# End of the layers of a transformer encoder with routed experts: adds of stored expert outputs moved, last blocks shared by four engines, a square in halves

## Chip, cores and metric

One core of a Trainium2 chip (trn2) runs the whole program in one launch. The metric is the device time of one execution in microseconds (us). The engines are named as in the profile: PE (TensorE; PEld its weight loads), DVE (VectorE), ACT (ScalarE), POOL (GpSimd) and SP (SyncE, which only issues transfers here). Everything is float32.

## What is computed

Two layers over 512 tokens of width 1024, then a final RMSNorm. What matters here is how a layer ends:

```python
for l in range(DEPTH):
    ...
    x = x + g1 * hybrid_mixer(h, ...)
    h = rms_norm(x, norm2[l]) * (1.0 + sc2) + sh2
    x = x + g2 * grouped_moe(h.reshape(B * S, D), w_router, router_bias,
                             w1[l], w3[l], w2[l]).reshape(B, S, D)
return rms_norm(x, norm_f)
```

`grouped_moe` sends each token to two of 16 experts and adds their two outputs with weights `gw`. The next layer begins with `rms_norm(x, norm1)`.

## The kernel before

The tokens are four blocks `t` of 128 rows; `x[:, t, :]` is 128 x 1024. The routed part of a layer runs in eleven passes (`PASSES`) of 128 token places each. In a pass PE multiplies gathered tokens with w1 and w3 of the pass's experts (`up_tiles`, L2130), ACT and DVE form the hidden values, PE transposes them (`hidden_transposes`, L2116) and multiplies by w2 (`down_tiles`, L2141) in two halves of 512 columns, into banks 6 and 7. DVE scales each half by `g2` into `ysb` (`put_out`, L1637) and counts it on `y_e`. For passes 0 to 9 POOL scatters `ysb` to the array `ys_d` in HBM, two rows for each token. When the scatters have landed, SP loads `ys_d` back, 1 MB for each block, into `cy[t]` (`load_outputs`, L773): blocks 0 and 1 into `reg_a`, 2 and 3 into `reg_b`. DVE adds them to `x` with the weights (`add_output`, L1185: one scalar_tensor_tensor of 128 x 1024 for each of the two outputs; `add_outputs` is both).

The last pass isn't stored. PE adds it straight from `ysb` by a product with a matrix `last_t` that holds places and weights (`last_pass`, L1757), into the banks that `last_bank` names.

- After layer 0, DVE adds these banks to `x` (`add_last_pass`, L1199) and ACT squares block after block for the norm of layer 1 (`square`, L934; `root`, L938). DVE makes mean squares (`mean_square`, L1173), reciprocals (L1178) and the scaled rows `xn` (L1180), which PE transposes (L1775).
- After layer 1, PE also adds `x` itself by a product with the identity (L1756), so the final `x` of a block lies in two banks. ACT squares each half there (L1151), DVE works out the mean square (L1704, L1707), ACT the root (L938), DVE the reciprocal (L1709) and the two scaled halves (L1713), and SP stores the block (L802). `fx_s` tells PE that a block of `x` is ready.

All orders are written out by hand: each engine has one program, in which it waits on counting semaphores. The order of DVE at the end of a layer is that of its last step (`e == PASSES`): the stored outputs of block 0, the two halves of the last down product, then (layer 0 only) one stored output of block 1. A conditional piece (`extra_blocks`) for routings that overflow the passes stands between the passes and the last adds on every engine; with these inputs none of its instructions runs, only the branch. PE waits for both halves of `y_e` ahead of that branch.

## Time and profile before

| | |
|---|---|
| median of 3 runs | 1547.74 us (1547.10 to 1547.87) |
| the profiled execution's own time | 1547.94 us |
| its span, first to last instruction | 1546.0 us |
| mean granted TensorE clock | 0.982 |
| PE busy | 1461.4 us, 95% of the span |
| DVE, ACT, POOL busy | 615.0, 427.2 and 87.1 us (40%, 28%, 6%) |
| chain of waits that ended last | PE 87%, DMA 6%, DVE 3%, ACT 2%, issue 1% |
| moved by the transfer engines | 346.8 MB, mean 224 GB/s |

The profile is of one execution. The chain of waits follows the last instruction back to whatever released it, so its shares say on what the end hung. All times in the rows are from the start of the span. Layer 0 ends around 770 to 782 us, layer 1 at 1518 to 1546 us.

### The profile page before, as it was taken

Reading aid. Unit: us, or ns where it says so; the run is one execution under the profiler, and the core shown is the slowest. Engines: PE = TensorE matmul, PEld = TensorE weight load, DVE = VectorE, ACT = ScalarE, POOL = GpSimd, SP = SyncE. Lnnn points to the kernel's source line nnn. Section 1 sums busy time; section 2 is a strip of 40 time slices with the busy share of each in tenths; the row PEclk is TensorE's granted clock in tenths of the full one; section 3 lists DMA queues with packets and bytes.
Section 4 is the critical chain, followed back from the end, with each engine's and each line's share of the span. In section 5 each row is a group of like instructions: output and inputs, shape, how many; then the busy total and the mean of one; then the engine's idle time right before and its main releaser. Section 6 shows DMA issues by size and latency. Waiting matters only on the chain.

```text
span 1546.0 us, 19921 instructions
## 1 busy us (share of the span) xinstructions
PE 1461.4 (95%) x7688; PEld 797.8 (52%) x7689; DVE 615.0 (40%) x1395; ACT 427.2 (28%) x988; POOL 87.1 (6%) x96
## 2 busy tenths in 40 slices
PE   4998999999999799999899899999999969999997
PEld 1565555677754443343346555666776433333333
DVE  0377554565742511111165774464333251111115
ACT  1427565300011211111141565541000122111112
POOL 0000002000000101100000000110000010111000
PEclk8999999999999799999999999999999979999999
DMA  9626073225282799999972703401303368999994
GB/s 361 243 84 247 2 247 107 83 67 151 65 316 97 287 372 392 421 419 422 375 272 109 243 35 122 151 1 41 109 1 152 148 231 340 407 408 420 424 413 188
DMA packets 94874, 346.80 MB, mean 224 GB/s; under 512 B 13738, under 2 KB 37898, under 8 KB 80376
## 3 DMA queue, kind: packets, MB, share of 16 engines
q1 hardware_dynamic: 69152, 305.68, 50.8%
q0 software_dynamic: 8976, 31.40, 5.5%
q10 hardware_dynamic: 16648, 8.40, 1.9%
q8 instruction: 63, 1.03, 0.3%
q14 instruction: 35, 0.29, 0.1%
HBM read 331.55 MB, written 21.00 MB: 228 GB/s over the span
## 4 chain that ended last, share of the span: by engine, by line
PE 87%; DMA 6%; DVE 3%; ACT 2%; issue 1%; DVEq 0%; SPq 0%; POOLq 0%; ACTq 0%
PE bank L2130 18%; PE bank L1868 13%; PE bank L1811 10%; PE bank L2141 9%; PE bank L2036 7%; PE bank L1910 7%; PE bank L1925 5%; PE bank L1935 4%; PE bank L1945 4%; DMA ring<-in_w 3%; PE bank L1851 2%; PE bank L1775 2%; DMA ring<-in_w_ada 1%; PE bank L1740 1%; PE bank L2096 1%
## 5 line engine op out<-in xcount | busy, mean ns | idle before, releaser
L2130 PE MATMUL bank<-ring,reg_b 128*32 128x512 f32 (+2 forms) x1312 | 269.0, 602 | 2.1 <-ACT reg_b L1113 2.1
L1811 PE MATMUL bank<-ring,hT 128*128 128x512 f32 (+3 forms) x512 | 158.9, 471 | 2.4 <-ACT hT L946 2.4
L2130 PEld LDWEIGHTS bank<-ring,reg_b 128*32 128x32 f32 (+2 forms) x1312 | 86.4, 125 | 139.7 <-issue 136.9
L2141 PE MATMUL bank<-ring,reg_b 128*32 128x512 f32 (+2 forms) x768 | 141.5, 594 | 6.8 <-DMA ring<-in_w 5.4
L1811 PEld LDWEIGHTS bank<-ring,hT 128*128 128x128 f32 x512 | 97.7, 192 | 59.0 <-issue 32.2
L1910 PE MATMUL bank<-reg_a,ring 128*128 128x512 f32 x256 | 112.6, 593 | 0.9 <-issue 0.9
L2036 PE MATMUL bank<-ring,reg_b 128*128 128x512 f32 x256 | 113.0, 596 | 0.0
L1113 ACT ACTIVATE reg_b<-bank,cur 128x128 f32<-128x128 f32 x176 | 64.0, 470 | 164.9 <-PE bank L2096 164.9
L1025 ACT ACTIVATE reg_f<-bank,nmax 128x512 f32<-128x512 f32 x128 | 87.2, 684 | 57.2 <-DVE nmax L1337 56.1
L1337 DVE TENSOR_REDUCE nmax<-bank 128x1 f32<-128x512 f32 x128 | 83.7, 685 | 47.9 <-PE bank L1925 47.7
L2141 PEld LDWEIGHTS bank<-ring,reg_b 128*32 128x32 f32 (+2 forms) x768 | 47.6, 123 | 78.7 <-issue 76.1
L1868 PE MATMUL bank<-hT,ring 128*128 128x256 f32 x384 | 88.1, 379 | 0.0
L1637 DVE TENSOR_TENSOR reg_d<-bank,reg_c 128x512 f32<-128x512 f32 x44 | 30.3, 691 | 138.5 <-PE bank L2141 138.5
L2130 PE MATMUL bank<-hT,reg_b 128*32 128x512 f32 (+2 forms) x288 | 84.6, 593 | 0.0
L1868 PEld LDWEIGHTS bank<-hT,ring 128*128 128x128 f32 x384 | 72.8, 190 | 15.8 <-issue 6.7
L1945 PE MATMUL bank<-cst,reg_f 128*128 128x128 f32 x512 | 71.8, 282 | 7.9 <-DVE reg_f L1331 5.1
L1625 DVE TENSOR_TENSOR reg_b<-bank,reg_b 128x512 f32<-128x512 f32 x22 | 15.2, 692 | 159.0 <-ACT reg_b L1120 159.0
L1910 PEld LDWEIGHTS bank<-reg_a,ring 128*128 128x128 f32 x256 | 48.5, 190 | 55.6 <-issue 54.9
L2036 PEld LDWEIGHTS bank<-ring,reg_b 128*128 128x128 f32 x256 | 47.7, 190 | 56.3 <-issue 56.3
L1331 DVE TENSOR_SCALAR reg_f<-reg_f,linv 128x512 f32<-128x512 f32 x128 | 66.2, 517 | 10.3 <-issue 0.4
L1945 PEld LDWEIGHTS bank<-cst,reg_f 128*128 128x128 f32 x512 | 55.4, 142 | 28.1 <-DVE reg_f L1331 18.8
L1630 DVE TENSOR_TENSOR reg_b<-bank,reg_b 128x512 f32<-128x512 f32 x22 | 15.2, 692 | 123.6 <-PE bank L2130 123.6
(305 smaller groups left out, 1832.8 us busy)
## 6 DMA issues: line engine op xcount, KB each, us to landing
ring<-in_w SPq DMA_DIRECT2D x72, 2048.0 KB, 15.4
ring<-in_w_ada SPq DMA_DIRECT2D x19, 2048.0 KB, 11.8
reg_a<-in_w SPq DMA_DIRECT2D x12, 2048.0 KB, 12.7
hT<-in_w SPq DMA_DIRECT2D x12, 2048.0 KB, 15.6
ring<-in_w_in SPq DMA_DIRECT2D x10, 2048.0 KB, 19.3
vb<-in_w_ada ACTq DMA_DIRECT2D x16, 512.0 KB, 3.9
ring<-in_w_o SPq DMA_DIRECT2D x4, 2048.0 KB, 8.1
ring<-in_w_proj_a SPq DMA_DIRECT2D x8, 512.0 KB, 10.7
```

What stands on the lines that cost most here:

```text
L1025: A(prob[:, u % 2, h, :], bank[4 + at][:, :], ACT.Exp, bias=nmax[:, at:at + 1], accum_out=lsum[:, at:at + 1]).then_inc(ex_s, 1)
L1113: ins = A(xsT[:, b, cc, :], bank[(p0 + k) % 2][:, c * P:(c + 1) * P], ACT.Identity, scale=scale2(cc), bias=shift2(cc))
L1331: TS(prob[:, u % 2, h, :], prob[:, u % 2, h, :], linv[:, at:at + 1], None, ALU.mult).then_inc(pn_s, 1)
L1337: v.tensor_reduce(nmax[:, at:at + 1], bank[4 + at][:, :], X, ALU.max, negate=True).then_inc(mx_s, 1)
L1811: ins = pe.matmul(bank[z_bank(k)][:, 0:n], hT[:, c, t * P:(t + 1) * P], w[:, c, :], start=c == 0, stop=c == NC - 1)
L1868: ins = pe.matmul(bank[bk][:, half * 256:(half + 1) * 256], w[:, c, :], tokens[:, c, :], start=c == 0, stop=c == 3)
L1910: ins = pe.matmul(branch_bank(j, q)[:, :], w[:, c, (j % 4) * P:(j % 4 + 1) * P], oT[:, c + 4 * q, :], start=c == 0, stop=c == 3)
L1925: pe.matmul(bank[4 + 2 * (u % 2) + h][:, :], q_of(k, h), k_of(k, h), start=True, stop=True).then_inc(s_r, 1)
L1945: ins = pe.transpose(bank[2 + h][:, kc * P:(kc + 1) * P], prob[:, u % 2, h, kc * P:(kc + 1) * P], ident)
L2036: ins = pe.matmul(wo_bank(k)[:, :], mT[:, c, t * P:(t + 1) * P], w[:, c, :], start=c == 0, stop=c == NC - 1)
L2130: ins = pe.matmul(bank[bk][at:at + n, :], xsT[:, p % 2, c, at:at + n], slot(MOE_SLOT[j, m], NC, F)[:, c, :], start=c == 0, stop=c == NC - 1)
L2141: ins = pe.matmul(bank[6 + h][at:at + n, :], uT[:, c, at:at + n], slot(MOE_SLOT[j, 2], 4, D)[:, c, h * 512:(h + 1) * 512], start=c == 0, s ...
```

## The change

1. The stored outputs of block 0 are added between the two halves of the last down product (in the last layer those of block 1 too, after them), where they stood ahead of both halves.
2. PE's wait for `ysb` is taken per half, inside `last_pass`, and stands behind the branch.
3. In the last layer only blocks 0 and 2 get `x` through the identity product; for both halves this stands ahead of the two `last_t` products. In blocks 1 and 3 DVE adds the banks to `x` (`final_add`). Block 3's stored outputs are weighted by ACT (in place), summed and added to `x` by POOL. Block 3 is loaded ahead of block 2.
4. Of the final scaling ACT does three halves (block 0, and half 0 of block 2), whose gain POOL multiplies in; DVE does the other five. The last block is stored in two halves.
5. In the norm at the start of layer 1, block 0 is squared in two halves, the first as soon as its half of `x` is there.

```diff
 def last_bank(layer, t):
-    return ((6, 2, 6, 6) if layer < DEPTH - 1 else (6, 2, 4, 0))[t]
+    return ((6, 2, 6, 6) if layer < DEPTH - 1 else (2, 4, 0, 6))[t]
 ...
 # SP
-                for t in range(2, NT):
+                for t in (2, 3) if l < DEPTH - 1 else (3, 2):
                     load_outputs(t, cg_s[t])
 ...
+            t = NT - 1
+            for h in range(2):
+                cols = slice(h * 512, (h + 1) * 512)
+                wait(sp, out_s[t], h + 1)
+                sp.dma_start(out[0, t * P:(t + 1) * P, cols], xn[:, t, cols]).then_inc(out_st, 16)
 ...
 # POOL
+                if l == DEPTH - 1:
+                    both = cy[NT - 1]
+                    wait(pool, fw_s, 2)
+                    pool.tensor_tensor(both[:, 0, :], both[:, 0, :], both[:, 1, :], ALU.add).then_inc(fp_s, 1)
+                    wait(pool, fp_s, 1)
+                    pool.tensor_tensor(x[:, NT - 1, :], x[:, NT - 1, :], both[:, 0, :], ALU.add).then_inc(fp_s, 1)
+                    wait(pool, fp_s, 2)
                 extra_blocks(pool, rows_beyond(pool, l), n_ov, n_tab, body, new_table)
                 pool.sem_inc(ov_all, 1)
+            for n, (t, h) in enumerate(((0, 0), (0, 1), (2, 0))):
+                cols = slice(h * 512, (h + 1) * 512)
+                wait(pool, fy_s, n + 1)
+                pool.tensor_tensor(xn[:, t, cols], xn[:, t, cols], nf_row[:, cols], ALU.mult).then_inc(out_s[t], 1)
 ...
 # ACT
+                    if l > 0 and t == 0:
+                        act.wait_ge(xh_s, l)
+                        A(sq_j[:, 0:512], x[:, t, 0:512], ACT.Square, accum_out=ssq_h[:, 0:1]).then_inc(sqz_s, 1)
+                        act.wait_ge(x2, l * NT + 1)
+                        A(sq_j[:, 512:D], x[:, t, 512:D], ACT.Square, accum_out=ssq[:, t:t + 1]).then_inc(sq_s, 1)
 ...
+                if l == DEPTH - 1:
+                    act.wait_ge(cg_s[NT - 1], l * 16 + 16)
+                    for k in range(2):
+                        A(cy[NT - 1][:, k, :], cy[NT - 1][:, k, :], ACT.Identity, scale=gw[:, k, NT - 1:NT]).then_inc(fw_s, 1)
                 extra_blocks(act, most, n_ov, n_tab, body)
             warm_root(DEPTH + 1)
 ...
             for t in range(NT):
-                for h, (total, done) in enumerate(((lsum, sqh_s), (ssq, sq_s))):
-                    act.wait_ge(lp_r, ((DEPTH - 1) * NT + t) * 2 + h + 1)
-                    A(sq_j[:, h * 512:(h + 1) * 512], bank[last_bank(DEPTH - 1, t) + h][:, :], ACT.Square,
-                      accum_out=total[:, t:t + 1]).then_inc(done, 1)
+                for h in range(2):
+                    final_square(t, h)
+                    if t == 3 and h == 0:
+                        final_scale(2, 0)
                 root(2 * DEPTH, t)
+                if t == 0:
+                    for h in range(2):
+                        final_scale(0, h)
 ...
 # DVE
-                    else:
-                        add_outputs(l, 0)
-                        out_before()
-                        if l < DEPTH - 1:
-                            add_output(l, 1, 0)
+                    elif l < DEPTH - 1:
+                        out_before((0,))
+                        add_outputs(l, 0)
+                        out_before((1,))
+                        add_output(l, 1, 0)
+                    else:
+                        add_outputs(l, 0).then_inc(fx_s, 1)
+                        out_before((0,))
+                        add_outputs(l, 1)
+                        out_before((1,))
 ...
+            add_outputs(DEPTH - 1, 2).then_inc(fx_s, 1)
+            final_add(1, 0)
+            final_root(0)
+            final_add(1, 1)
+            final_root(1)
+            v.drain()
+            for h in range(2):
+                final_out(1, h)
+            v.wait_ge(fp_s, 2)
+            final_add(3, 0)
+            final_root(2)
+            final_add(3, 1)
+            v.drain()
+            final_out(2, 1)
+            final_root(3)
+            v.drain()
+            for h in range(2):
+                final_out(3, h)
 ...
 # PE, last_pass
-                for h in range(2):
-                    cols = slice(h * 512, (h + 1) * 512)
-                    own = layer == DEPTH - 1
-                    dst = bank[last_bank(layer, t) + h][:, :]
-                    if own:
-                        pe.matmul(dst, ident, x[:, t, cols], start=True, stop=False)
-                    pe.matmul(dst, last_t[:, t, :], ysb[:, 0, cols], start=not own, stop=True).then_inc(lp_r, 1)
+                if own:
+                    for h in range(2):
+                        pe.matmul(dst[h], ident, x[:, t, cols[h]], start=True, stop=False)
+                for h in range(2):
+                    if t == 0:
+                        pe.wait_ge(y_e, (layer * PASSES + PASSES) * 2 - 1 + h)
+                    pe.matmul(dst[h], last_t[:, t, :], ysb[:, 0, cols[h]], start=not own, stop=True).then_inc(lp_r, 1)
```

`own` is true for blocks 0 and 2 of the last layer. `final_square(t, h)` squares a half from its bank (even `t`) or from `x` (odd `t`); `final_root(t)` is the mean square, the wait for ACT's root and the reciprocal as before; `final_out(t, h)` is the scaling by reciprocal and gain, from `x` for odd `t` and from the bank for even `t`; `final_scale(t, h)` is ACT's scaling by the reciprocal alone.

DVE at the very end of the last layer, before (L1185 stored outputs, L1637 halves of the last down product, L1704 to L1713 the norm of block 0):

```order
L1185 SCALAR_TENSOR_TENSOR x<-reg_a,gw,x 128x1024 [waits token_outputs_loaded0] x2
L1637 TENSOR_TENSOR reg_d<-bank,reg_c 128x512 [waits expert_out_ready,expert_out_stored0]
L1637 TENSOR_TENSOR reg_d<-bank,reg_c 128x512 [waits expert_out_ready]
...
L1185 SCALAR_TENSOR_TENSOR x<-reg_a,gw,x 128x1024 [waits token_outputs_loaded1] x2
L1185 SCALAR_TENSOR_TENSOR x<-reg_b,gw,x 128x1024 [waits token_outputs_loaded2] x2
L1704 TENSOR_SCALAR lsum<-lsum 128x1 [waits square_sum_of_first_half]
L1707 TENSOR_SCALAR ssq<-ssq,lsum 128x1 [waits square_sums]
L1709 RECIPROCAL rstd<-ssq 128x1 [waits roots]
L1713 SCALAR_TENSOR_TENSOR reg_a<-bank,rstd,reg_c 128x512 x2
L1185 SCALAR_TENSOR_TENSOR x<-reg_b,gw,x 128x1024 [waits token_outputs_loaded3] x2
```

And now (L1249 stored outputs, L1703 halves, L1772 `final_add`, L1777 to L1782 `final_root`, L1788 `final_out`):

```order
L1249 SCALAR_TENSOR_TENSOR x<-reg_a,gw,x 128x1024 [waits token_outputs_loaded0] x2
L1703 TENSOR_TENSOR reg_d<-bank,reg_c 128x512 [waits expert_out_ready,expert_out_stored0]
L1249 SCALAR_TENSOR_TENSOR x<-reg_a,gw,x 128x1024 [waits token_outputs_loaded1] x2
L1703 TENSOR_TENSOR reg_d<-bank,reg_c 128x512 [waits expert_out_ready]
...
L1249 SCALAR_TENSOR_TENSOR x<-reg_b,gw,x 128x1024 [waits token_outputs_loaded2] x2
L1772 TENSOR_TENSOR x<-bank4,x 128x512 [waits last_pass_added_up]
L1777 TENSOR_SCALAR lsum<-lsum 128x1 [waits square_sum_of_first_half]
L1780 TENSOR_SCALAR ssq<-ssq,lsum 128x1 [waits square_sums]
L1782 RECIPROCAL rstd<-ssq 128x1 [waits roots]
L1772 TENSOR_TENSOR x<-bank5,x 128x512 [waits last_pass_added_up]
```

The pair for block 1 went between the halves, the pair for block 3 left DVE, and two adds from banks came in.

PE at the same place, before (L1756 identity, L1757 last pass; each row is one half of a block, block 0 and the start of block 1 shown; the branch waits for `expert_out_read`, which is `y_e`):

```order
L533 COMPARE_AND_BRANCH [waits expert_out_read]
...
L1756 MATMUL bank6<-x,cst 128x512 [waits final_x_in_sbuf,last_pass_weights_copied]
L1757 MATMUL bank6<-reg_d 128x512
L1756 MATMUL bank7<-x,cst 128x512
L1757 MATMUL bank7<-reg_d 128x512
L1756 MATMUL bank2<-x,cst 128x512 [waits final_x_in_sbuf]
```

And now (L1849 identity, L1853 last pass; block 0 in banks 2 and 3, block 1 in 4 and 5, block 2 in 0 and 1; block 3 follows):

```order
L541 COMPARE_AND_BRANCH
...
L1849 MATMUL bank2<-x,cst 128x512 [waits final_x_in_sbuf,last_pass_weights_copied]
L1849 MATMUL bank3<-x,cst 128x512
L1853 MATMUL bank2<-reg_d 128x512 [waits expert_out_read]
L1853 MATMUL bank3<-reg_d 128x512 [waits expert_out_read]
L1853 MATMUL bank4<-reg_d 128x512
L1853 MATMUL bank5<-reg_d 128x512
L1849 MATMUL bank0<-x,cst 128x512 [waits final_x_in_sbuf]
L1849 MATMUL bank1<-x,cst 128x512
L1853 MATMUL bank0<-reg_d 128x512
...
```

The sixteen half-block products became twelve, and the wait for `ysb` moved from the branch to the products that read it.

DVE between the layers, now (L1263 the last pass's halves into `x`, L1231 and L1234 the mean square of block 0 in two steps; before it was one step, L1173, and nothing stood between the two halves of L1637):

```order
L1703 TENSOR_TENSOR reg_d<-bank,reg_c 128x512 [waits expert_out_ready,expert_out_stored0]
L1249 SCALAR_TENSOR_TENSOR x<-reg_a,gw,x 128x1024 [waits token_outputs_loaded0] x2
L1703 TENSOR_TENSOR reg_d<-bank,reg_c 128x512 [waits expert_out_ready]
L1249 SCALAR_TENSOR_TENSOR x<-reg_a,gw,x 128x1024 [waits token_outputs_loaded1]
...
L1263 TENSOR_TENSOR x<-bank,x 128x512 [waits last_pass_added_up] x2
L1249 SCALAR_TENSOR_TENSOR x<-reg_a,gw,x 128x1024 [waits token_outputs_loaded1]
L1231 TENSOR_SCALAR ssq_h<-ssq_h 128x1 [waits square_sum_of_first_half_after_moe]
L1234 TENSOR_SCALAR ssq<-ssq,ssq_h 128x1 [waits square_sums]
```

The stored outputs of block 0 now follow the first half; the rest keeps its place.

## Rows read from the trace of the kernel before

**Rows 1.** Chain of waits, last 30 us (start us, us, what).

```profile
1517.88 7.15 PE bank L2141 x16
...
1525.06 0.08 DVE reg_d L1637
...
1525.28 0.52 DVEq L1697
...
1526.17 1.10 PE bank L1756 x2
...
1539.28 0.87 PE bank L1757 x2
...
1540.18 0.70 ACT reg_f L1151 x2
```

**Rows 2.** Timeline, end of layer 1 (start us, us, engine, line, out<-in, count).

```profile
1517.85 1.28 ACT L961 ACT_TABLE_LOAD   x1
...
1521.69 0.69 DVE L1637 TENSOR_TENSOR reg_d<-bank,reg_c 128x512 f32<-128x512 f32 x1 [0.48 <-PE bank L2141]
...
1525.88 2.64 DVE L1185 SCALAR_TENSOR_TENSOR x<-reg_a,gw,x 128x1024 f32<-128x1024 f32 x2
...
1533.27 2.63 DVE L1185 SCALAR_TENSOR_TENSOR x<-reg_b,gw,x 128x1024 f32<-128x1024 f32 x2
...
1541.62 1.41 DVE L1713 SCALAR_TENSOR_TENSOR reg_a<-bank,rstd,reg_c 128x512 f32<-128x512 f32 x2
```

**Rows 3.** Chain of waits between the layers and in layer 1.

```profile
807.00 43.25 PE bank L1811 x148
...
1469.53 7.05 PE bank L2130 x64
...
1477.89 23.60 DMA ring<-in_w
```

**Rows 4.** Timeline between the layers.

```profile
767.88 2.41 PE L2141 MATMUL bank<-ring,reg_b 128*128 128x512 f32 x5 [0.69 <-ACT reg_b L1125]
...
771.99 2.65 DVE L1185 SCALAR_TENSOR_TENSOR x<-reg_a,gw,x 128x1024 f32<-128x1024 f32 x2 [5.51 <-DMA reg_a<-ys_d]
...
774.56 1.28 DVE L1637 TENSOR_TENSOR reg_d<-bank,reg_c 128x512 f32<-128x512 f32 x2
...
776.32 3.70 PE L1757 MATMUL bank<-reg_d 128*128 128x512 f32 x8 [1.30 <-DVE reg_d L1637]
...
777.03 0.16 DVE L1216 COPY gain<-gain_n 128x8 f32<-128x8 f32 x1
...
778.34 0.69 DVE L1199 TENSOR_TENSOR x<-bank,x 128x512 f32<-128x512 f32 x1 [0.17 <-PE bank L1757]
...
778.95 1.28 DVE L1185 SCALAR_TENSOR_TENSOR x<-reg_a,gw,x 128x1024 f32<-128x1024 f32 x1
...
780.25 0.15 DVE L1173 TENSOR_SCALAR ssq<-ssq 128x1 f32<-128x1 f32 x1
```

**Rows 5.** Transfers: issue of the loads of blocks 2 and 3, and us to landing of both.

```profile
1515.86 0.80 SPq L773 DMA_DIRECT2D reg_b<-ys_d  x2
...
DMA to landing us min/median/max: 8.2/9.3/10.3
```

**Rows 6.** Timeline, POOL and DVE in layer 1's attention.

```profile
1004.73 0.49 DVE L1331 TENSOR_SCALAR reg_f<-reg_f,linv 128x512 f32<-128x512 f32 x1
...
1004.79 2.63 POOL L849 TENSOR_TENSOR ring<-hT,ring 128x1024 f32<-128x1024 f32 x1 [0.18 <-POOL hT L847]
...
1005.59 2.12 DVE L1331 TENSOR_SCALAR reg_f<-reg_f,linv 128x512 f32<-128x512 f32 x1
...
1007.60 2.34 POOL L851 TENSOR_TENSOR ring<-hT,ring 128x1024 f32<-128x1024 f32 x1 [0.18 <-POOL ring L849]
```

**Rows 7.** Line L1104 on ACT: durations in ns min/median/max, first and last start.

```profile
L1104 ACT ACTIVATE reg_a<-x,rstd x2: 1132/1132/1132, 504.4 to 1253.7; 128x1024 f32<-128x1024 f32 x2
```

**Rows 8.** Transfers, final stores: KB each, median us to landing.

```profile
out<-reg_a SPq DMA_DIRECT2D x4, 512.0 KB, 2.6
```

More of the change, by code:

```diff
@@ L513, in trunk @@
         ov_all = sem("extra_pass_done")
-        out_s = sem("out_ready")
+        out_s = [sem(f"out_block_{t}_ready") for t in range(NT)]
         out_st = sem("out_stored")
@@ L799, in _ @@
                 wait(sp, y_r, (l * PASSES + PASSES) * 2)
-            for t in range(NT):
-                wait(sp, out_s, t + 1)
+            for t in range(NT - 1):
+                wait(sp, out_s[t], 2)
                 sp.dma_start(out[0, t * P:(t + 1) * P, :], xn[:, t, :]).then_inc(out_st, 16)
-            wait(sp, out_st, 16 * NT)
+            t = NT - 1
[3 more added lines that the diff above has]
+                sp.dma_start(out[0, t * P:(t + 1) * P, cols], xn[:, t, cols]).then_inc(out_st, 16)
+            wait(sp, out_st, 16 * (NT + 1))
         @block.gpsimd
@@ L1171, in mean_square @@
             def mean_square(base, t):
+                if base in range(2, 2 * DEPTH, 2) and t == 0:
+                    v.wait_ge(sqz_s, base // 2)
+                    TS(ssq_h[:, 0:1], ssq_h[:, 0:1], 1.0 / D, EPS, ALU.mult, ALU.add)
+                    v.drain()
+                    v.wait_ge(sq_s, base * NT + (t + 1))
+                    TS(ssq[:, t:t + 1], ssq[:, t:t + 1], 1.0 / D, ssq_h[:, 0:1], ALU.mult, ALU.add).then_inc(ms_s, 1)
+                    return
                 v.wait_ge(sq_s, base * NT + (t + 1))
@@ L1630, in hidden, with put_out @@
                     TT(u_s, bank[5][:, :], u_s, ALU.mult).then_inc(u_s_s, 1)
-                def put_out(f, p):
-                    for n in range(2):
+                def put_out(f, p, halves=(0, 1)):
+                    for n in halves:
                         v.wait_ge(y_r, (l * PASSES + f) * 2 + (n + 1))
@@ L1694, in _ @@
                 extra_blocks(v, most, n_ov, n_tab, body, new_table, finish=add_extra)
[L1697 to L1714 removed]
+                v.drain().then_inc(xe_s, 1)
@@ new lines, in final_add, with final_root @@
+            def final_add(t, h):
+                v.wait_ge(lp_r, ((DEPTH - 1) * NT + t) * 2 + h + 1)
+                cols = slice(h * 512, (h + 1) * 512)
+                TT(x[:, t, cols], bank[last_bank(DEPTH - 1, t) + h][:, :], x[:, t, cols], ALU.add).then_inc(fa_s, 1)
+            def final_root(t):
+                v.wait_ge(sqh_s, DEPTH + t + 1)
+                TS(lsum[:, t:t + 1], lsum[:, t:t + 1], 1.0 / D, EPS, ALU.mult, ALU.add)
+                v.drain()
+                v.wait_ge(sq_s, 2 * DEPTH * NT + t + 1)
+                TS(ssq[:, t:t + 1], ssq[:, t:t + 1], 1.0 / D, lsum[:, t:t + 1], ALU.mult, ALU.add).then_inc(ms_s, 1)
+                v.wait_ge(rt_s, 2 * DEPTH * NT + (t + 1))
+                v.reciprocal(rstd[:, t:t + 1], ssq[:, t:t + 1]).then_inc(fr_s, 1)
@@ L1746, in last_pass @@
                     pe.wait_ge(wt_s, layer + 1)
[L1747 to L1749 removed]
+                own = layer == DEPTH - 1 and t % 2 == 0
+                if own:
+                    pe.wait_ge(fx_s, t // 2 + 1)
+                elif layer < DEPTH - 1 and t >= 2:
                     pe.wait_ge(x2, (layer + 1) * NT + (1 if t == 2 else 3))
[L1751 to L1757 removed]
+                dst = [bank[last_bank(layer, t) + h][:, :] for h in range(2)]
+                cols = [slice(h * 512, (h + 1) * 512) for h in range(2)]
+                if own:
+                    for h in range(2):
+                        pe.matmul(dst[h], ident, x[:, t, cols[h]], start=True, stop=False)
+                for h in range(2):
+                    if t == 0:
+                        pe.wait_ge(y_e, (layer * PASSES + PASSES) * 2 - 1 + h)
+                    pe.matmul(dst[h], last_t[:, t, :], ysb[:, 0, cols[h]], start=not own, stop=True).then_inc(lp_r, 1)
             pe.wait_ge(clr_s, 1)
```

66 lines of the change are left out of this document (39 added, 27 removed).

## The prediction

> **What bounds the kernel now.** I read the page's totals, then the chain of waits, then the timelines of the two places that the change touches, last the transfers and POOL. PE is busy for 95% of the span and carries 87% of the chain, so only what takes work or a wait off PE's path, or shortens the tail behind PE, can count. At the end of layer 1 [rows 1] the reader is to see four things. The last down product takes 7.15 us from 1517.88. PE then does nothing until 1526.17: DVE still reads the second half (to 1525.75), and PE's branch stands behind the wait for it. Sixteen half-block products of 0.86 us follow without a gap, to 1540.15. A tail of ACT and DVE for the last block ends it at 1543.03 [rows 1, 2]; one store of 512 KB, 2.6 us to landing [rows 8], and the close of the program reach 1546.0. Between the layers [rows 4] PE ends its last-pass products at 780.02 and then waits for DVE and ACT, which go through two adds from the banks, a square, mean, root and scaling; the mean square ends at 780.40. From 807 on PE is the chain [rows 3], and of the late loads the longest, 23.60 us from 1477.89, is issued when PE's product at 1469.53 has ended. So an earlier start of layer 1 moves the loads with it, and I carry a gain there in full to the end.
>
> **Between the layers.** DVE's first half of the down product is ready at about 771.7 (767.88 and the 3.81 us that layer 1 has from the product's start to DVE's read, 1517.88 to 1521.69 [rows 1, 2]), so it goes ahead of the stored outputs at no cost but 0.3 us on a pair that has slack until 775.0. The second half then starts at 775.06 and ends at 775.75, against the pair's end at 775.84 [rows 4]. PE has its branch behind it and the first half's `ysb`, so its products start at 775.0 to 775.4, not at 776.32, and both halves are done when DVE has copied its gains (777.19, less 0.1). DVE's two adds, the second of which waited for PE until 778.34, run back to back from 777.15 to 778.46; before they ended at 779.03: 0.57 us. The split square ends some 0.8 us after the adds, about 779.3, where the whole one ended just ahead of DVE's step at 780.25; but DVE still has the stored output of block 1 in front of the mean square (1.28 us from 778.95, now from 778.38 to 779.66), then two small steps of 0.15 and 0.22 in place of one. The mean square is there at 780.02, not 780.40. Everything behind waits for it: **0.38 us gained**. Bounds: 0.1 (PE's products come late after all) and 0.6 (the adds' gain in full).
>
> **The last layer, with no engine disturbing another.** The second down half isn't delayed: block 0's pair ends at 1521.2, the first half takes 1521.69 to 1522.38 [rows 2], block 1's pair 2.64 us, to 1525.0, and the second half is ready at 1525.03. PE needs only `x` of block 0 for its identity products, so they start when the down product has been issued. I take 1525.0; the branch, 0.42 us from 1525.75 to 1526.17 in rows 1, could push it to 1525.4. Twelve products of 0.86 end at 1535.5, against 1540.15. But the loads set a second date: block 3's outputs land 8.2 us after 1515.86, at 1524.06, block 2's at 1516.24 + 10.3 = 1526.54 [rows 5]. DVE's pair for block 2 then runs to 1529.2; PE wants it at 1530.2. Then DVE and ACT are the path. Block 1's first half is added by 1530.3, block 0's root and reciprocal end at 1531.1, ACT scales block 0 to 1532.4 (two of about 0.65) and squares block 1 to 1533.7; root and reciprocal to 1534.3, DVE's two halves of block 1 to 1535.7 (0.67 each from SBUF), the add of block 3's first half to 1536.35, block 2's mean, root and reciprocal to 1537.2, the second add to 1537.8, DVE's half of block 2 to 1538.65. ACT meanwhile squares and scales to 1538.95, and mean, root, reciprocal and two halves end at **1541.0**. That is 2.0 us before 1543.03. The gain on PE (4.6 us) is not on the path by then: DVE is late next. It gives up one pair (2.6 us) and three scalings (0.7 each), but takes four adds from banks (0.7 each), and it still waits for ACT's root four times.
>
> **The last store.** Its second half is 256 KB. A load of 1 MB behind another took 2.1 us longer [rows 5] (10.3 - 8.2, issued 0.4 apart, so 2.5 for 1 MB), so 256 KB less are worth about 0.6 us; I take **0.45**, with bounds of 0 and 0.7.
>
> **What POOL takes back.** ACT weights block 3's outputs in two steps of 1.13 us [rows 7] from 1524.06, done at about 1526.25; POOL then runs two adds of 128 x 1024, 2.34 us each [rows 6]. Rows 6 show what that does to DVE: a tensor_scalar on SBUF takes 0.49 us, but the one that starts at 1005.59 under POOL's add takes 2.12 and ends 0.3 us after the add; POOL's own add, begun under a DVE instruction, takes 2.63 in place of 2.34. One holds the other off for a whole instruction. No row shows the form at stake here, a scalar_tensor_tensor that reads two tensors in SBUF (DVE's pair for block 2), so its hold lies between 0 and all of POOL's time; I take it as held, since the nearest row is. The Trainium skill (SBUF — State Buffer, Who interferes with whom) says that a DVE instruction with two SBUF inputs contends with a GpSimd instruction that reads SBUF, as an exclusive lock; by it the hold is certain (the rows don't show this form), and the adds from a bank, with one SBUF input, go free. If the two alternate once, the pair for block 2 ends at 1531.2 instead of 1529.2, and what hung at 1529.6 moves by 1.6 us. POOL's gain products (about 1.2 us each, half of 2.34) then touch DVE's scaling of block 1, 0.3 more. **1.9 us lost**, DVE ends at 1542.9.
>
> **Sum.** -0.38 - 2.0 - 0.45 + 1.9 = -0.9 us, against the profiled execution's 1547.94: 1547.0. The median of the runs is 0.2 below that execution, so the forecast is 1546.8.
>
> **Rivals.**
> - *No hold.* POOL and DVE don't meet: 1547.74 - 2.85 = 1544.9. For it: rows 6 show only a single-tensor instruction held. Against: they show no SBUF-reading DVE instruction that ran through a POOL add. A further 0.3 from PE's early start, a full 0.7 at the store or 0.6 between the layers takes it past 0.2%.
> - *Held twice, slower than before.* POOL's first add starts at about 1526.4, 0.15 us before block 2 has landed. It decides here: if POOL is first, DVE's first step of the pair waits until 1528.7 and ends at 1529.8; POOL's second add, waiting since 1528.9, slips in before the second step, which ends at 1533.2. PE's products for block 2 start 3 us late, DVE's chain 3.6 us; POOL is out of the way afterwards. End of DVE 1544.45: 1547.74 + 1.4 - 0.45 - 0.38 = 1548.3. For it: the dates above. Against: 0.15 us is within what landings move, and the gap between the pair's two steps is under 0.1 us. Past 0.2% it would take another 2.5 us, as by small DVE steps held too (1.6 us each time).
> - *The early start doesn't come about.* PE's branch and waits hold its products until after 1526. Then the end loses up to 1 us only where nothing is held: 1545.9.
>
> **How the numbers follow.** About 0.2% (3.1 us) is what a measurement of this kernel can tell from no change. Forecast 0.45, no hold 0.27, held twice 0.18, late start 0.06, the rest for mishaps of either sign. The range reaches from the no-hold case with its bounds, 1544.3, to held twice with the late bounds, 1549.0. Faster by over 0.2% is half of the no-hold case: 0.14. Slower by over 0.2%: 0.04. Within: 0.82.
>
> **What would show it.** Between the layers: DVE's two adds back to back, and the mean square about 0.4 us sooner after the down product's start. At the end: identity products at 1525 on the old clock; POOL's first add beside DVE's pair for block 2, one step of which takes over 2 us; DVE's last scaling 25.0 us after the down product's start (25.15 before), 23.1 with no hold, 26.6 if held twice. It would be wrong if DVE's pair takes 2.6 us under POOL's add, if the last store gains nothing, or if PE's stretch in layer 1 changes length.

## The result, and the profile after

| | before | after |
|---|---|---|
| median of the runs | 1547.74 us | 1552.71 us |
| lowest to highest, 7 runs each | 1547.10 to 1550.81 | 1551.12 to 1557.37 |
| ratio after / before | | 1.0031, 95% interval 1.0019 to 1.0043 |
| profiled execution, its span | 1547.94 / 1546.0 us | 1557.37 / 1555.6 us |

The change makes the kernel slower by 5.0 us, 0.31%. The forecast was 1546.8 with a range up to 1549.0, and it gave 0.04 to slower by over 0.2%: it was wrong in sign, and the time lies outside its range. In the comparisons below three executions that took 1691 to 4807 us (two of e2, one of e10b) are left out.

The profiled execution of after is the slowest of its seven, so it has to be read by pieces. All times below are counted from the start of a layer's **last down product** (before 767.88 and 1517.88, after 772.56 and 1523.52). Ahead of the first of these after is 4.7 us late, in stages that the diff leaves as they were: PE waited 3.30 us for a weight load there (1.79 in before's trace) and ran slowly for some microseconds. The medians are 5.0 apart, not 9.4, and e3 below, which has the same code there, waited 1.78 us; so I count that piece as one of this execution, not of the change.

Timeline of after, PE, the wait ahead of the change:

```profile
754.60 0.62 PE L2237 MATMUL bank<-ring,reg_b 128*32 128x512 f32 x2 [3.30 <-DMA ring<-in_w]
```

**Between the layers.** Timeline of after (columns as in [rows 4]):

```profile
772.56 7.13 PE L2237 MATMUL bank<-ring,reg_b 128*128 128x512 f32 x16 [0.69 <-ACT reg_b L1156]
779.53 3.79 PE L1853 MATMUL bank<-reg_d 128*128 128x512 f32 x8
...
782.06 1.29 DVE L1263 TENSOR_TENSOR x<-bank,x 128x512 f32<-128x512 f32 x2
...
784.68 0.21 DVE L1234 TENSOR_SCALAR ssq<-ssq,ssq_h 128x1 f32<-128x1 f32 x1
...
786.21 1.97 PE L1871 MATMUL bank<-cst,reg_a 128*128 128x128 f32 x8 [2.89 <-DVE reg_a L1244]
...
787.98 2.53 PE L1853 MATMUL bank<-reg_d 128*128 128x512 f32 x4
```

and the same place in before:

```profile
781.72 1.16 PE L1775 MATMUL bank<-cst,reg_a 128*128 128x128 f32 x8 [1.70 <-DVE reg_a L1180]
782.72 1.88 PE L1757 MATMUL bank<-reg_d 128*128 128x512 f32 x4
```

PE's first last-pass products come 6.97 us after the down product's start (8.44 before, [rows 4]), DVE's two adds run back to back (1.29 us), the mean square is there at 784.90, 12.34 us after the start, against 12.52. That is what was forecast (0.38 us), if smaller: 0.18 us. But PE has the same work done earlier and waits for DVE for 2.89 us, where it waited 1.70, and its next eight transposes take 1.97 us, not 1.16, and the four products 2.53, not 1.88. Windows of after (us, busy times of the engines with counts, granted clock of PE, DMA):

```profile
784.56:786.06 1.50, 0.00 (x0) 0.00 (x0) 1.07 (x4) 0.20 (x1) 0.00 (x0) 0.93 1.08 363
786.06:787.56 1.50, 1.35 (x7) 1.35 (x8) 1.24 (x5) 0.13 (x1) 0.00 (x0) 0.50 1.06 373
787.56:789.06 1.50, 1.50 (x5) 0.98 (x5) 1.50 (x2) 1.50 (x5) 0.00 (x0) 0.50 1.06 371
789.06:790.56 1.50, 1.50 (x4) 0.68 (x4) 1.43 (x2) 1.50 (x5) 0.00 (x0) 0.93 1.08 381
```

The granted clock is 0.50 behind the gap (the 1.2 GHz level; 2.4 GHz is 1.00), where in before the eight transposes and four products ran in the times of a clock of 1.00. Layer 1's first product with weights is at 790.51 in the chain of waits, 17.95 us after the down product's start; in before it was at 784.60, 16.72. So this place **loses 1.23 us** in this execution.

**The last layer.** Timeline of after; SPq rows are DMA issues:

```profile
1529.38 2.19 ACT L1179 ACTIVATE reg_b<-reg_b,gw 128x1024 f32<-128x1024 f32 x2 [5.92 <-DMA reg_b<-ys_d]
1530.49 1.88 PE L1849 MATMUL bank<-x,cst 128*128 128x512 f32 x4
...
1531.76 2.34 POOL L931 TENSOR_TENSOR reg_b<-reg_b 128x1024 f32<-128x1024 f32 x1 [14.85 <-ACT reg_b L1179]
...
1532.77 5.69 DVE L1249 SCALAR_TENSOR_TENSOR x<-reg_b,gw,x 128x1024 f32<-128x1024 f32 x2 [1.39 <-DMA reg_b<-ys_d]
...
1534.27 3.10 POOL L933 TENSOR_TENSOR x<-x,reg_b 128x1024 f32<-128x1024 f32 x1 [0.18 <-POOL reg_b L931]
...
1538.51 1.98 PE L1849 MATMUL bank<-x,cst 128*128 128x512 f32 x4 [2.71 <-DVE x L1249]
...
1543.65 5.35 SPq L810 DMA_DIRECT2D out<-reg_a  x3
...
1547.32 1.26 POOL L941 TENSOR_TENSOR reg_a<-reg_a,reg_c 128x512 f32<-128x512 f32 x1 [3.76 <-ACT reg_a L1200]
...
1548.52 1.41 DVE L1788 SCALAR_TENSOR_TENSOR reg_a<-x,rstd,reg_c 128x512 f32<-128x512 f32 x2
1549.37 0.99 SPq L815 DMA_DIRECT2D out<-reg_a  x2
```

PE starts block 0 at 6.97 us after the down product's start (8.29 before, [rows 1]): the early start came. DVE's pair for block 2, 2.64 us where nothing disturbs it, takes 5.69. The chain of waits shows how (start us, us, what):

```profile
1521.87 10.88 DMA reg_b<-ys_d
1532.75 0.03 issue
1532.77 2.41 DVE x L1249
...
1535.25 3.21 DVE x L1249
```

POOL's first add had begun at 1531.76, 1 us before block 2 landed; DVE's first step waits it out and ends at 1535.18, POOL's second add slips in, and DVE's second step ends at 1538.46. DVE's last scaling ends at 1549.93, 26.41 us after the down product's start, against 25.15: **1.26 us lost**. (The trace shows that DVE's steps end behind POOL's adds; that POOL holds DVE is read from the lengths here and tested in e4.)

**The close.** What each engine's end-of-program drain shows in after (durations in ns min/median/max, first and last start in us):

```profile
L208 POOLq DRAIN  x1: 8084/8084/8084, 1547.3 to 1547.3; - x1
...
L208 SPq DRAIN  x1: 13/13/13, 1552.7 to 1552.7; - x1
```

and in before:

```profile
L208 POOLq DRAIN  x1: 7027/7027/7027, 1511.0 to 1511.0; - x1
...
L208 SPq DRAIN  x1: 13/13/13, 1545.8 to 1545.8; - x1
```

SP's drain marks the last store's landing. In before the program ends 0.2 us later. In after POOL is not done then: its drain starts when its last product is issued (1547.3), includes that product (1.26 us) and goes on 6.8 us more, to 1555.4, and the program waits. From DVE's last scaling to the end of the span it is 5.67 us, 2.97 in before: **2.70 us lost**. Nor do the halves of the last store gain anything here: 2.8 us from DVE's end to SP's drain, as before.

The sum is 1.23 + 1.26 + 2.70 = 5.2 us, less 0.27 in layer 1's stretch (from the first product, 790.51, to the last down product 733.01 us, 733.28 before), against the 5.0 us between the medians. Each of these pieces is read from one execution of each kernel; the first of them does not come in every execution, as e3 shows below, so that the sum meets the medians this closely is in part luck.

### The profile page after: what moved, and what is told of

Its sections match the earlier page's. It is cut to its first block, busy times and chain, and to the rows that moved or that the text cites. A ratio compares the mean times of both kernels' runs of the same rounds, so it can differ in the third digit from the quotient of the medians.

```text
span 1555.6 us, 19927 instructions
## 1 busy us (share of the span) xinstructions
PE 1461.6 (94%) x7680; PEld 798.0 (51%) x7681; DVE 616.9 (40%) x1395; ACT 431.7 (28%) x995; POOL 96.3 (6%) x101
## 4 chain that ended last, share of the span: by engine, by line
PE 86%; DMA 6%; DVE 3%; ACT 2%; issue 1%; DVEq 0%; SPq 0%; POOLq 0%; ACTq 0%
PE bank L2226 18%; PE bank L1964 12%; PE bank L1907 10%; PE bank L2237 9%; PE bank L2132 7%; PE bank L2006 7%; PE bank L2021 5%; PE bank L2031 4%; PE bank L2041 4%; DMA ring<-in_w 3%; PE bank L1947 2%; PE bank L1871 2%; DMA ring<-in_w_ada 1%; PE bank L1833 1%; PE bank L2192 1%
## 5 line engine op out<-in xcount | busy, mean ns | idle before, releaser
L1703 DVE TENSOR_TENSOR reg_d<-bank,reg_c 128x512 f32<-128x512 f32 x44 | 30.4, 692 | 145.0 <-PE bank L2237 144.8
```

## Experiments

Every run below was timed beside the kernel before. Ratios are to before. "Filler" is two products on PE that nobody needs, shown under e13.

| run | what it is | ratio, 95% interval |
|---|---|---|
| after | | 1.0031, 1.0019 to 1.0043 |
| e1, e14 | before + the part between the layers | 1.0008, 0.9997 to 1.0019; 1.0015, 1.0004 to 1.0025 |
| e13 | e1 + filler on PE | 1.0002, 0.9993 to 1.0012 |
| e2 | after, the part between the layers undone | 1.0022, 1.0013 to 1.0031 |
| e3 | after, no late product on POOL | 1.0016, 1.0007 to 1.0024 |
| e4 | after, POOL waits for DVE's pair | 1.0014, 1.0005 to 1.0023 |
| e5 | before + one tiny late product on POOL | 1.0029, 1.0018 to 1.0040 |
| e6 | before + one late wait on POOL | 1.0023, 1.0014 to 1.0033 |
| e7 | e3 and e4 together | 1.0000, 0.9990 to 1.0009 |
| e8 | e7 + filler | 0.9990, 0.9981 to 0.9999 |
| e9b | e8, POOL does its two adds alone | 0.9983, 0.9974 to 0.9991 |
| e10b | e9b without the filler | 0.9999, 0.9989 to 1.0008 |
| e11b | after + filler | 1.0032, 1.0020 to 1.0044 |
| e12b | before + last store in halves | 0.9999, 0.9990 to 1.0007 |

### The close of the program: e3, e5, e6

Theory: POOL needs 6.8 to 7 us to close behind whatever it did last. Rival: the stores at the end, 1 MB in a row on the queue. e3 takes the product for block 2, POOL's last, off POOL:

```diff
-            for n, (t, h) in enumerate(((0, 0), (0, 1), (2, 0))):
+            for n, (t, h) in enumerate(((0, 0), (0, 1))):
...
-                    if t == 3 and h == 0:
-                        final_scale(2, 0)
...
+            final_out(2, 0)
             final_out(2, 1)
```

> The changed kernel, but DVE scales half 0 of block 2, so that POOL's last instruction is the gain product of block 0's second half. Theory (the program ends with POOL's drain, 6.8 us after POOL's last arithmetic): POOL's drain ends before the last store has landed, the span ends 0.3 us after that landing (3 us after it in the changed kernel), DVE ends 0.5 us later; in all 2.1 us below the changed kernel, 2.9 above the kernel before. Rival (the end of the program is late for another reason, such as the two half stores): the 3 us stay and the time is 5 us above.

Drains of e3:

```profile
L208 POOLq DRAIN  x1: 9062/9062/9062, 1534.2 to 1534.2; - x1
...
L208 SPq DRAIN  x1: 13/13/13, 1545.6 to 1545.6; - x1
```

POOL is closed at 1543.3 and the span ends at 1545.9, 0.3 us after the landing. DVE has one step more and the hold is still there (pair 5.71 us), so DVE ends 27.3 us after the down product's start, 0.9 us later than in after where 0.5 was expected; the time falls from 1.0031 to 1.0016, 2.3 us. e5 and e6 put the cost alone on the kernel before, whose stores they leave as they are:

```diff
                 pool.sem_inc(ov_all, 1)
 
+            wait(pool, out_s, 4)
+            pool.tensor_tensor(kr[:, 0, 0:8], kr[:, 0, 0:8], kr[:, 0, 8:16], ALU.mult)
```

(e6 has the wait alone.)

> The kernel before, with one thing more: at its end POOL waits until all four blocks are scaled and then does one product of 128 x 8 elements, which nobody needs. Theory (POOL closes only some 6.8 us after its last instruction; the profile of after has a drain of 8.08 us from 1547.3, 1.26 us of it the product): POOL's drain ends at about 1543.1 + 0.1 + 6.8 to 7 = 1550.0, the program ends there, 4 us later than before (ratio about 1.0026). Rival (what after loses at its end comes from the 1 MB of stores that stand in a row on the queue): the time stays at that of before, 1.000, since the stores are not touched and the small product is done long before the last store has landed.

> As e5, but POOL only waits, and does no product. If it is the arithmetic that the drain waits out, POOL's drain is short or starts 7 us before the end unseen, and the time is that of before (1.000); if the drain of POOL takes 7 us whatever it did last, the end comes at 1543.1 + 7.0 = 1550.1, 4 us later (1.0026). I give the second 0.6, since before drains for 7.03 us after an instruction that also moved nothing large.

POOL's product and drain in e5:

```profile
1545.00 0.20 POOL L919 TENSOR_TENSOR kr<-kr 128x8 f32<-128x8 f32 x1 [31.94 <-DVE reg_a L1716]
```

```profile
L208 POOLq DRAIN  x1: 7009/7009/7009, 1545.0 to 1545.0; - x1
L208 SPq DRAIN  x1: 13/13/13, 1547.6 to 1547.6; - x1
```

and POOL's drain in e6:

```profile
L208 POOLq DRAIN  x1: 6769/6769/6769, 1540.7 to 1540.7; - x1
```

A product of 0.2 us that nobody needs costs 4.5 us (0.29%), and a bare wait costs nearly as much (0.23%), with stores untouched: the rival falls. From DVE's last scaling to the end of the span the profiles have 7.4 us in e5 and 7.1 in e6, 2.97 in before. The 6.8 to 7.0 us lie behind POOL's last instruction, of either kind; what POOL does in them stays open. In the kernel before, POOL's drain of 7.03 us begins at 1511.0 and is over by 1518, unseen.

### POOL and DVE: e4

```diff
                     wait(pool, fw_s, 2)
+                    wait(pool, fx_s, 2)
                     pool.tensor_tensor(both[:, 0, :], both[:, 0, :], both[:, 1, :], ALU.add).then_inc(fp_s, 1)
```

> The changed kernel, but POOL begins its two adds only when DVE's pair of block 2 is done. Theory (DVE's pair is held off by POOL's adds): the pair takes 2.6 us instead of 5.7, PE starts block 2's products at once, and DVE's last scaling ends 24 to 25 us after the start of the last down product (26.4 in the changed kernel), since POOL's gain products now meet DVE's scaling of block 1. POOL's drain still ends the program: 1.5 to 2.5 us below the changed kernel, 2.5 to 3.5 above the kernel before. Rival (the pair is slow by itself, beside the loads): it stays at 5.7 us.

Timeline of e4:

```profile
1530.77 2.64 DVE L1250 SCALAR_TENSOR_TENSOR x<-reg_b,gw,x 128x1024 f32<-128x1024 f32 x2 [1.78 <-DMA reg_b<-ys_d]
...
1533.60 2.35 POOL L932 TENSOR_TENSOR reg_b<-reg_b 128x1024 f32<-128x1024 f32 x1 [19.08 <-DVE x L1250]
...
1536.13 2.35 POOL L934 TENSOR_TENSOR x<-x,reg_b 128x1024 f32<-128x1024 f32 x1 [0.18 <-POOL reg_b L932]
```

With nothing else changed the pair is back at 2.64 us and both adds at 2.35. DVE ends at 1544.93, 23.80 us after its down product's start of 1521.13 (26.41 in after, 24 to 25 expected). POOL is now later, its three products end at 1543.72, and its drain still ends the program. The ratio of 1.0014 says 2.6 us gained, as 26.41 - 23.80 does. The Trainium skill (SBUF — State Buffer, Who interferes with whom) calls the pair of ports that DVE and GpSimd share "an exclusive lock" and names a DVE instruction with two SBUF inputs among those that contend. It adds that "issue order, not op shape, decides who blocks". The traces agree with the lock: 5.69 us under POOL's adds (5.71 in e3, 5.82 in e2, 6.62 in e11b), 2.64 without (e4, e7, e8, e9b). On the order they show one side only: POOL's first add began ahead of DVE's pair in all four, by 1.01 us in after and by 0.08 in e11b, and DVE waited each time; no run has DVE's pair begin first under POOL's adds.

### The clock between the layers: e1, e2, e13, e14

e1 and e14 are one kernel, before with this part of the change alone; e2 is after without it:

```diff
-                        out_before((0,))
-                        add_outputs(l, 0)
-                        out_before((1,))
+                        add_outputs(l, 0)
+                        out_before()
                         add_output(l, 1, 0)
...
-                    if l > 0 and t == 0:
+                    if False:
...
-                if base in range(2, 2 * DEPTH, 2) and t == 0:
+                if False:
...
+                if l < DEPTH - 1:
+                    pe.wait_ge(y_e, (l * PASSES + PASSES) * 2)
+
                 def extra_added():
```

> The kernel before with the change's part between the layers alone. Theory (the longer idle of PE lets its clock fall): PE's first transposes of layer 1 run at the granted clock 0.5, as in the changed kernel (eight in 1.97 us, not 1.16), the first product of layer 1 starts 17.9 us after the start of the last down product of layer 0 (16.7 before), and the time is 0.8 to 1.2 us above the kernel before. Rival (the prediction's step): 16.3 us, and 0.4 us below.

> The changed kernel with the order, the waits and the whole square of before between the layers. Theory: 16.7 us from the last down product of layer 0 to layer 1's first product, clock 1.0 there, about 1.2 us below the changed kernel, so 3.8 us above the kernel before. Rival (the loss lies in the unchanged stages, whose loads came later in the changed kernel's profile): still 5 us above.

In e1's profile the theory failed at first. PE waited 2.76 us and no clock fell (the eight transposes took 1.16 us, layer 1's first product stood 16.39 us after the down product, 0.33 under before):

```profile
781.60 1.16 PE L1797 MATMUL bank<-cst,reg_a 128*128 128x128 f32 x8 [2.76 <-DVE reg_a L1195]
```

After and e4 (gaps of 2.89 and 2.9 us) did show the fall, and both had also run at half clock some 25 us before, so I thought the two falls linked. e13 is e1 with the filler; it puts two products behind the first two blocks' last ones, into a bank that nobody reads:

```diff
                     last_pass(l - 1, 1)
+                    for _ in range(2):
+                        pe.matmul(bank[5][:, :], ident, ysb[:, 0, 0:512], start=True, stop=True)
                 norm_transposes(TR_N1, 0, 0)
```

> Before with the part between the layers and the two filler products alone. Theory (of six profiled executions with a gap of 2.8 to 3.1 us between the layers, the three that had run at half clock some 25 us earlier, behind a wait for a load at 752 to 755, ran at half clock behind the gap too, and the other three did not; with the filler none of three did): the first product of layer 1 starts 16.3 to 16.4 us after the last down product (16.72 before, 17.9 with the fall) whatever the load did, and the ratio is 0.9997. Rival (the filler does nothing for the median): the same ratio as e14.

> The kernel of e1 a second time, beside e13 on the same chip. Theory: in a share of its executions the clock falls behind the gap, 1.5 us each time, so it lies 0.3 to 1.5 us above e13 and at 1.0000 to 1.0008 of before. In the profile: if PE waited over 2.3 us for the load at about 752, a granted clock of 0.5 behind the gap and 17.8 to 17.9 us to the first product; if under 2.0 us, a clock of 1.00 and 16.3 to 16.4 us. Rival: no difference from e13, or a fall without the early one.

Timeline of PE in e14, the same kernel as e1:

```profile
751.37 0.62 PE L2163 MATMUL bank<-ring,reg_b 128*32 128x512 f32 x2 [2.79 <-DMA ring<-in_w]
```

```profile
781.10 1.97 PE L1797 MATMUL bank<-cst,reg_a 128*128 128x128 f32 x8 [2.70 <-DVE reg_a L1195]
782.86 2.77 PE L1779 MATMUL bank<-reg_d 128*128 128x512 f32 x4
```

and its windows:

```profile
752.00:754.00 2.00, 2.00 (x25) 0.69 (x20) 0.00 (x0) 0.00 (x0) 0.00 (x0) 1.00 0.99 414
...
782.00:784.00 2.00, 2.00 (x7) 1.48 (x7) 2.00 (x3) 1.69 (x5) 0.00 (x0) 0.50 1.06 373
```

Timeline of PE in e13:

```profile
779.10 1.88 PE L1812 MATMUL bank<-reg_d,cst 128*128 128x512 f32 x4
781.95 1.16 PE L1797 MATMUL bank<-cst,reg_a 128*128 128x128 f32 x8 [0.97 <-DVE reg_a L1195]
782.94 1.88 PE L1779 MATMUL bank<-reg_d 128*128 128x512 f32 x4
```

In e14 the clock is 1.00 at 752 and 0.50 behind a gap of 2.70 us: the fall does not need an earlier one, and by the chain layer 1's first product is at 785.63, 18.00 us after the down product's start (767.63). In e13 it is at 784.83, 16.32 us after 768.51. The means of the 12 times of e14 and of e13 differ by 1.8 us (0.6 to 3.1 by resampling them); e10b against e9b, the same edit elsewhere, gives 2.4 (1.0 to 3.7), e7 against e8 1.0 (-0.1 to 2.1), and after against e11b, below, nothing (1.0031 and 1.0032). So the filler gains clearly in two of the four pairs. That it does so by the clock is shown in the profiles, one of each kernel, and argued for the medians.

Over all profiles: of the seven executions with a gap of 2.70 to 3.07 us (after, e1, e3, e4, e7, e10b, e14) four ran at 0.50 behind it (after, e4, e10b, e14); of the nine whose gap is before's 1.70 or is filled (0.97 to 1.78 left) (before, e2, e5, e6, e8, e9b, e11b, e12b, e13) none did. What decides among the seven stays open: e1 and e14 are one kernel with gaps of 2.76 and 2.70, and e3 and after have 2.89 both.

e2's profile has 16.70 us from the down product's start to the first product (before 16.72), as expected, and its time is 1.4 us below after's by the ratios (1.0022) where 1.2 was expected; the two intervals overlap, so the times alone don't show it.

### After with the filler alone: e11b

> After with nothing but the filler. Theory: the stretch between the layers is 0.2 to 0.3 us shorter than before's in every execution, with a clock of 1.00; the last layer (pair of 5.7 us, DVE's end 26.4 us after the down product's start) and POOL's drain are as in after; 3.5 to 4.2 us above before, ratio 1.0023 to 1.0027. Rival (the fall of the clock has nothing to do with that gap): as after, 1.0031, or a clock of 0.5 there in the profile.

The part between the layers is as expected (16.53 us, clock 1.00), and still the ratio is that of after (1.0032 where 1.0023 to 1.0027 was expected; the interval reaches down to 1.0020). The profile says where it went, in this execution: DVE's pair is held for 6.62 us, DVE ends 27.5 us after the down product's start, and PE's next gap has the fall of the clock instead.

```profile
1527.74 6.62 DVE L1249 SCALAR_TENSOR_TENSOR x<-reg_b,gw,x 128x1024 f32<-128x1024 f32 x2 [1.51 <-DMA reg_b<-ys_d]
...
1534.42 3.47 PE L1849 MATMUL bank<-x,cst 128*128 128x512 f32 x4 [3.76 <-DVE x L1249]
```

Four identity products take 3.47 us, not 1.88, at a granted clock of 0.50. e2 shows the same there (3.48 us behind 3.09 us of gap); after and e3, with gaps of 2.71 and 2.99 us at this place, kept 1.00. Whether that holds for the medians, one profile can't say.

### Both mendings, and a kernel that beats both: e7, e8, e9b, e10b, e12b

> After, with both mendings of the last layer: POOL's adds wait until DVE's pair for block 2 has ended, and DVE, not ACT and POOL, scales the first half of block 2; the part between the layers is after's. Theory: pair for block 2 takes 2.64 us, POOL's last arithmetic ends 8 us or more before the program's end, so its drain is hidden and the program ends 0.3 us after the last store's landing; DVE's last scaling ends 24.0 to 24.8 us after the last down product's start (before 25.15, after 26.41). Sum against before: between layers -0.3 (clock stays) or +1.2 (clock falls), end -0.4 to -1.1: ratio 0.999 to 1.000; clearly under after. Rival (the end holds something else, as the queue of stores): still 2 us or more above before.

> As e7, and PE does two products of 128 x 512 into a free bank, which nobody reads, behind the first two blocks' last products in the gap between layers (2.9 us long there, 1.7 in before). Theory (the clock falls when that gap is long, in some executions): the gap is 1.7 us again, PE's transposes start as in e7 and the clock is 1.00 in every execution there; the median is below e7's by 0 to 1.5 us, by the share of executions in which the clock fell. Rival (the fall comes from something that happens before, as the wait for a DMA at 754): no difference, or +0.1.

e7 (the diffs of e3 and e4) is level with before, e8 with the filler 0.10% under it. DVE ends 23.40 and 24.00 us after the down product's start, where 24.0 to 24.8 was expected. POOL's last product in e7 ends 7.0 us before the program does, not 8 or more, so its drain is only just hidden (to 1544.0, as the last landing). Between the layers e8 shows 1.00 but gains nothing (17.13 us to the first product): DVE waited 0.52 us for block 1's first stored output to land there, a second way in which that part depends on a load. And the stores now pile up, in e7 and in e8. Timeline of e8, SP's queue:

```profile
1538.25 1.65 SPq L810 DMA_DIRECT2D out<-reg_a  x3
1540.54 1.83 SPq L815 DMA_DIRECT2D out<-reg_a  x2
```

Block 0 waits for POOL's product (behind its adds), and blocks 1 and 2 stand behind block 0's store on SP's queue: 2 MB issued between 1538.25 and 1541.2, and the last landing is 3.8 us after DVE's end (1541.11 to 1544.9). POOL's drain ends at 1545.0 too. So e9b takes block 0 back from ACT and POOL and puts it where DVE waited 1.35 us for ACT's squares:

```diff
-            for n, (t, h) in enumerate(((0, 0), (0, 1))):
-                cols = slice(h * 512, (h + 1) * 512)
-                wait(pool, fy_s, n + 1)
-                pool.tensor_tensor(xn[:, t, cols], xn[:, t, cols], nf_row[:, cols], ALU.mult).then_inc(out_s[t], 1)
...
-                if t == 0:
-                    for h in range(2):
-                        final_scale(0, h)
...
             final_add(1, 1)
+            v.drain()
+            for h in range(2):
+                final_out(0, h)
             final_root(1)
```

> As e8 (both mendings and the filler), but the first block's scale and gain are DVE's in two scalar_tensor_tensor steps from the banks, between its second add for block 1 and block 1's root; ACT's scaling and POOL's product for it are gone, so that POOL's last instruction is its second add. Theory (POOL's drain and the pile of stores both end the program in e8): DVE's two steps, 1.41 us, lie where it waited 1.35 us for ACT's squares, so its last scaling ends 23.4 to 24.1 us after the last down product's start (24.00 in e8); POOL's drain ends at least 3 us before the program does; block 0's store goes out some 5 us earlier, and the last landing comes 2.2 us after DVE's last step, not 3.8; the program ends 1.5 us sooner than e8, about 2.7 us under before: ratio 0.998. Rival (DVE's two more steps are on its path): DVE ends 1.4 us later and the ratio is that of e8, 0.999.

> As e9 without the two filler products, so that PE's gap between the layers is 2.9 us again. Theory (the granted clock falls behind a long gap in some executions, at about 1.5 us each): median 0 to 1.5 us above e9, 0.5 by e7 against e8. Rival: the same time as e9, and the profile shows 1.00 behind the gap.

e9b's last rows:

```profile
1536.46 6.60 SPq L810 DMA_DIRECT2D out<-reg_a  x3
1544.36 0.99 SPq L815 DMA_DIRECT2D out<-reg_a  x2
```

```profile
L208 POOLq DRAIN  x1: 6911/6911/6911, 1539.5 to 1539.5; - x1
...
L208 SPq DRAIN  x1: 13/13/13, 1547.1 to 1547.1; - x1
```

DVE ends 24.03 us after the down product's start (1544.93 and 1520.90), the two steps cost nothing, the last landing is 2.2 us later and POOL closes 0.7 us before it, nearer than the 3 us that I had expected. e9b is 0.17% under before, 1546.07 against 1548.00 us in its own comparison: slightly better than both kernels, and 2.6 us for 2.7 expected. Against e8 (0.9990) the intervals overlap. e10b, without the filler, is level with before (0.9999); its profile shows the fall again, transposes of 1.97 us behind 2.88 us of gap.

e12b is the last store alone, in halves, on the kernel before:

```diff
+            t = NT - 1
+            for h in range(2):
+                cols = slice(h * 512, (h + 1) * 512)
+                wait(sp, out_s, NT + h)
+                sp.dma_start(out[0, t * P:(t + 1) * P, cols], xn[:, t, cols]).then_inc(out_st, 16)
...
+                        if u == NT - 1 and h == 0:
+                            ins.then_inc(out_s, 1)
```

> Before with nothing but the last block's store in two halves. The prediction put 0.45 us on it. Theory (halves gain where no other store is under way): the last landing comes 2.2 us after DVE's last scaling, as in e3, not 2.8, so 0.5 to 0.6 us are gained, ratio 0.9996, within what a comparison can tell; the profile has to show it. Rival (halves gain nothing): 2.8 us from DVE's end to SP's drain.

DVE ends at 1543.11 and SP's drain is at 1545.3:

```profile
L208 SPq DRAIN  x1: 13/13/13, 1545.3 to 1545.3; - x1
```

2.2 us, 0.6 less than before. In after those 0.6 are lost: block 2's 512 KB, held up by POOL's product, are issued 0.7 us ahead of the first half, and a half takes 2.6 us to landing. In e3, e9b and e12b, where that store is 1.7 to 1.9 us ahead, a half takes 2.0. That the distance makes the difference is read from these four, not tested by itself. The medians (0.9999) can't tell so little.

## Why the prediction was wrong

- **The close of the program: a term that the sum didn't have, and the largest error.** "One store of 512 KB, 2.6 us to landing [rows 8], and the close of the program reach 1546.0" took the close as a constant. The change gives POOL a product at 1547.3, its first late work, and 2.70 us follow; e5 and e6 show it with nothing else changed (4.5 and 3.6 us by their ratios). I costed POOL's gain products only by what they do to DVE (0.3). A view of the engines' drains in the trace of before would have shown 7.03 us from 1511.
- **What POOL takes back: wrong case chosen.** I took "alternate once" (pair for block 2 to end 4.65 us after its start, +1.9). What came was the rival *held twice*: POOL first, DVE's first step behind it, POOL's second add in between. That rival put DVE's end at 26.6 us after the down product's start; it is 26.41, and e3, e2 and e11b are held as well. The hold costs 2.6 us (26.41 - 23.80 in e4), not 1.9. "0.15 us is within what landings move" did not weigh against it: block 2 landed 9.23 us after the down product's start, block 3's outputs 5.86 (8.66 and 6.18 forecast), so POOL was 1 us ahead, not 0.15. In e3, e2 and e11b it was ahead by 1.00, 0.89 and 0.08 us. The dates had POOL first, it was so four times out of four, and the rival should have had more of the chance than the forecast.
- **Between the layers: the gain came, and a larger loss behind it.** Adds back to back and the early products were right; the mean square gained 0.18 us in after and 0.33 in e1 for 0.38 forecast. "Everything behind waits for it: **0.38 us gained**" failed, since PE's speed behind its wait isn't given: work moved ahead lengthened the wait from 1.70 to 2.7 to 3.1 us and in four of seven profiles the granted clock was 0.50 behind it, which takes 1.3 to 1.6 us (17.85 to 18.03 us to the first product, 16.39 to 16.71 without). e1 and e14 are above before (1.0008 and 1.0015, of which only the second is clear of 1), not 0.38 us under it.
- **No disturbing: right in kind, too large.** -2.0 us forecast (23.1 us with the other terms out); e7 has 23.40, e4 23.80, e8 24.00. DVE's pair for block 2 could begin there 8.67, 9.64 and 9.32 us after the down product's start, for 8.66 forecast, so the landing accounts for none of the gap in e7 and can account for most of it in the others.
- **The last store: size about right, place wrong.** 0.6 us in e12b for 0.45 forecast; nothing in after, where another store had been issued 0.7 us before.

Term by term, forecast and measured (after's profile, and e4's for the last layer without the hold): between the layers -0.38 and +1.23; the last layer undisturbed -2.0 and -1.35; the hold +1.9 and +2.61; the store -0.45 and 0; the close 0 and +2.70. The measured ones make +5.2 us, for 5.0 between the medians. The two parts of the last layer also add up in the times: without the hold -0.17%, without the late product -0.15%, and both (e7) -0.31%.

## What to carry to other kernels

An engine that was idle at the end of a program is not free there: look first at how long each engine's drain runs in the trace, and if POOL's drain runs 7 us as here, give POOL nothing, not even a wait, in the last 7 us. Where work is shared between POOL and DVE, date each against the other by the landings that release them, and if POOL's step can be first, make it wait (e4) or give it work that doesn't fall beside DVE's steps on two SBUF tensors. And when work is moved ahead of a PE wait, count what the longer wait does to PE's granted clock behind it; where two products that nobody needs fit into the gap, they can be worth more than the move (1.8 and 2.4 us in two pairs of kernels here, nothing in a third).

## What the runs showed of the hardware that was not expected

- POOL's end-of-program drain takes 6.8 to 7.0 us behind its last instruction, be that a product of 1.26 us (after), one of 0.20 (e5) or a wait (e6, 6.77). In the same profiles ACT's takes 0.24 and SP's 0.01.
- PE at 0.50 of its clock behind a wait of 2.7 to 3.1 us, in four of seven executions, in none of nine behind 1.8 or less at that place; e1 and e14, one kernel, differ. In the last layer gaps of 2.71 and 2.99 us left it at 1.00 (after, e3), 3.09 and 3.76 us did not (e2, e11b).
- A scalar_tensor_tensor pair of 2.64 us on two SBUF tensors takes 5.7 to 6.6 us beside two POOL adds (2.34 us each alone, 2.34 and 3.10 there).
- The halves of a store save 0.6 us where the 512 KB before them were issued 1.7 to 1.9 us ahead (e3, e9b, e12b) and nothing where it was 0.7 us (after).
